# Reading and writing every helper matmul from the last column to the first

## The reference

```
x = x + 1/2 * SwiGLU_1(RMSNorm(x))                       # width 2816
h = RMSNorm(x)
[qA|kA|vA|c_q|c_kv|k_rope|gate_A|gate_B] = h @ w_in      # 1184 columns and two gates of 1024
oA = sliding-window attention, 8 heads of 64, 2 key heads, ALiBi, a sink per head
oB = latent attention, 8 heads, query rank 256, key/value rank 128, rotary part of 32
x = x + (sigmoid(gate_A)*(oA @ w_branch_a) + sigmoid(gate_B)*(oB @ w_branch_b)) @ w_out
x = x + 1/2 * SwiGLU_2(RMSNorm(x))
```

## Time and profile before

| what | value |
|---|---|
| median of the runs | 1039.09 us (1038.88 to 1039.29) |
| the profiled execution's own time | 1040.34 us |
| its span, first to last instruction | 1038.5 us |
| TensorE busy with matmuls (PE) | 1032.4 us, 99%, 5648 records |
| TensorE weight loads (PEld, beside PE) | 891.7 us, 86%, 5648 records |
| VectorE (DVE) | 718.3 us, 69% |
| ScalarE (ACT) | 586.1 us, 56% |
| GpSimd (POOL) | 61.8 us, 6% |
| DMA | 187.53 MB, mean 181 GB/s, 51.0% of 16 engines on the main queue |
| granted TensorE clock, mean | 1.000 |

### The profile page before, as it was taken

The page is one execution under the profiler, slowest core; times in us unless marked ns, Lnnn a source line. Parts: engine busy times, 40 slices in busy tenths (PEclk is TensorE's granted clock), DMA queues, the critical chain, the costliest instruction groups (busy, mean ns, idle before and its releaser), DMA issues.

```text
span 1038.5 us, 15559 instructions
## 1 busy us (share of the span) xinstructions
PE 1032.4 (99%) x5648; PEld 891.7 (86%) x5648; DVE 718.3 (69%) x1132; ACT 586.1 (56%) x935; POOL 61.8 (6%) x71
## 2 busy tenths in 40 slices
PE   8999999999999999999999999999999999999998
PEld 7888888998888888888888888889988888888887
DVE  6766666668786876666687666666688868666665
ACT  6555454466963754554565455455678646454552
POOL 0052000121100000000000000001211000000000
PEclk9999999999999999999999999999999999999999
DMA  7665544455435455655445555534454346545541
GB/s 264 248 225 192 204 162 167 140 183 193 146 123 203 173 187 189 205 189 209 179 147 202 202 192 182 210 136 152 154 203 163 122 163 219 205 163 202 191 173 61
DMA packets 35269, 187.53 MB, mean 181 GB/s; under 512 B 4368, under 2 KB 4384, under 8 KB 20128
## 3 DMA queue, kind: packets, MB, share of 16 engines
q1 hardware_dynamic: 34992, 186.51, 51.0%
q0 software_dynamic: 240, 0.53, 0.2%
HBM read 185.98 MB, written 1.05 MB: 180 GB/s over the span
## 4 chain that ended last, share of the span: by engine, by line
PE 99%; DMA 1%; SPq 0%; DVE 0%; ACT 0%; issue 0%
PE ps L1369 96%; PE ps L1803 1%; PE ps L1393 1%; DMA w_raw<-in_w_ffn 1%; PE ps L1832 1%; PE ps L1868 0%; PE ps L1712 0%; PE ps L1704 0%; PE ps L1414 0%; DVE x_cols L999 0%; ACT w_hi L554 0%; SPq L318 0%; SPq L317 0%
## 5 line engine op out<-in xcount | busy, mean ns | idle before, releaser
L1369 PE MATMUL ps<-hT,w_hi 128*128 128x512 f32 x1408 | 341.3, 391 | 1.9 <-ACT w_hi L554 1.9
L1369 PEld LDWEIGHTS ps<-hT,w_hi 128*128 128x128 f32 x1408 | 258.9, 188 | 52.4 <-ACT w_hi L554 2.1
L884 DVE TENSOR_TENSOR w_lo<-w_raw,w_hi 128x2048 fp32r<-128x2048 f32 x82 | 188.0, 2293 | 87.7 <-ACT w_hi L549 87.7
L1369 PEld LDWEIGHTS ps<-hT,w_lo 128*128 128x128 f32 x1408 | 176.8, 188 | 7.5
L1369 PE MATMUL ps<-hT,w_lo 128*128 128x256 f32 x1408 | 178.3, 279 | 0.0
L1369 PE MATMUL ps<-w_hi,hT 128*128 128x512 f32 (+2 forms) x576 | 174.3, 377 | 0.0
L549 ACT ACTIVATE w_hi<-w_raw 128x2048 fp32r<-128x2048 f32 x85 | 162.0, 1906 | 13.9 <-PE ps L1369 13.2
L1369 PE MATMUL ps<-w_lo,aTh 128*128 128x512 f32 x352 | 137.2, 390 | 0.0
L1369 PE MATMUL ps<-w_hi,aTl 128*128 128x512 f32 x352 | 137.0, 389 | 0.0
L1369 PE MATMUL ps<-w_hi,aTh 128*128 128x512 f32 x352 | 136.8, 390 | 0.0
L578 ACT ACTIVATE S<-ps 128x256 f32<-128x256 f32 x88 | 33.7, 383 | 154.6 <-PE ps L1369 154.6
(11 more groups left out here) (168 smaller groups left out, 952.9 us busy)
## 6 DMA issues: line engine op xcount, KB each, us to landing
w_raw<-in_w_ffn SPq DMA_DIRECT2D x85, 1024.0 KB, 4.9
w_raw<-in_w_ffn SPq DMA_DIRECT2D x90, 512.0 KB, 5.7
w_raw<-in_w_gate SPq DMA_DIRECT2D x16, 1024.0 KB, 5.1
w_raw<-in_w_proj SPq DMA_DIRECT2D x16, 592.0 KB, 4.4
w_raw<-in_w_branch SPq DMA_DIRECT2D x8, 1024.0 KB, 4.8
w_raw<-in_w_out SPq DMA_DIRECT2D x8, 1024.0 KB, 4.8
w_raw<-in_w_uq SPq DMA_DIRECT2D x4, 384.0 KB, 3.0
w_raw<-in_w_ffn SPq DMA_DIRECT2D x4, 256.0 KB, 6.6
```

What stands on the lines that cost most here:

```text
L884: dve.tensor_tensor(wl_gu[b], raw_gu[b], wh_gu[b].bitcast(F32), ALU.subtract).then_inc(lo_gu.sem, 1)
L1369: return pe.matmul(dst, w, m, start=start, stop=stop, skip_group_check=True)
```

## The change

The helper gives both the output and the moving operand with their columns in descending order. Column j of the moving operand still yields column j of the output, so each output element is the same sum; the stationary operand, the flags, the order of the matmuls and all waits are as before.

```diff
             def mm(dst, w, m, start, stop):
-                return pe.matmul(dst, w, m, start=start, stop=stop, skip_group_check=True)
+                return pe.matmul(dst[:, ::-1], w, m[:, ::-1], start=start, stop=stop, skip_group_check=True)
```

## The result

The changed kernel takes 1059.96 us (1059.67 to 1060.25) where the kernel before takes 1039.09 (1038.88 to 1039.29): a ratio of 1.0198, with a 95% interval of 1.0181 to 1.0215. That is 20.9 us slower. The forecast of no change was wrong. The time lies inside the range, but only because the range took in the second rival, a small price at each matmul.

A forecast was written before the change was run, and what follows sets the result against it. TensorE, busy in 99% of the span, was taken to bound the kernel. Read, write and fixed price summed as 0 + 0 + 0 on the median of 1039.09, giving 1039.1 us, with a range of 1035 to 1111 us.

The forecast's parts named there:

- the second rival: At each matmul, a small fixed price such as a refetch at the far end: 1075 us at 7 ns, 1111 at 14; chance 0.12.
- The bound: Whole kernel: TensorE, busy in 99% of the span, sets the time; any change per helper matmul arrives in full.
- Step (a): Helper matmuls' moving operand read downwards from SBUF: taken as zero, since aligned groups of neighbouring words stay complete.
- the third rival: In the matmul stream, turned order avoids a clash with weight load or other engines' writes: 28 us gain at most, 1011 us; chance 0.04.
- Step (b): Helper matmuls writing and adding downwards in PSUM: taken as zero, upper bound 0.35 ns more a column.
- The rule set against it: PSUM writes: lines hold two float32 values and non-contiguous patterns slow matmuls significantly; if step -1 counts, the sum is about 1820 us.
- Step (c): Fixed price per matmul for a start at the far end: taken as zero, 0 to 14 ns kept for the range.
- The first: At every helper matmul, descending SBUF reads or PSUM writes are not merged, each column its own access: about 1820 or 1930 us; chance 0.16.
- The fourth: In the build, both sides could be put back into ascending order, so nothing changes: 1039 us; chance 0.05, within the 0.68.

The follow-up runs named there:

- read_only: Kernel before, with only the moving operand read in descending column order and the output written upwards: 1060.17 us, ratio 1.0194.
- pairs_turned: Full kernel, moving operand and output upwards in pairs of columns, only the two columns of each pair swapped: 1039.52 us, ratio 1.000.
- quads_down: Full kernel, moving operand and output in groups of four columns in descending order, ascending inside each group: 1060.62 us, ratio 1.0202.
- write_only: Kernel before, with only the output written in descending column order and the moving operand read upwards: 1039.91 us, ratio 1.0001.
- micro_shift: Small kernel of 48-matmul sections, stationary operand shifted by 0 to 128 columns, then moving by 4, 32, 120; 512 up at stationary shift 64: 227.7 ns.
- micro_scan: Small kernel of 48-matmul sections, stationary operand shifted by 0 to 60 columns in steps of 4; 512 up: 226.7 ns at shift 0, 227.3 at 60.

## Why the prediction was wrong, step by step

**The bound** was right. TensorE passed every nanosecond on: 5000 float32r matmuls, no cover, no new wait.

**Step (a), the read, failed.** It was taken as zero and is the whole of the 20.9 us (read_only alone, 1.0194). The ground for zero was geometry: aligned groups stay whole. The runs support the half of it that concerns the inside of a group (pairs_turned, 1.000). But the order in which the groups are visited has a price (quads_down, 1.0202), and the argument looked at the moving stream alone. What it left out is the place of the stationary operand, and with it, by inference, the second read of the same engine, the weight load of 188 ns that runs beside each matmul. Rival 2 mentioned it as reading the same memory in its own order; that half sentence named what the runs on place point at, and the rival got 0.12 because it was argued away by the fixed part being alike for all operands. By the sizes in the code it was alike because the operands of all 512-wide matmuls lie at the same distance modulo 64 columns.

**The slope and the fixed part were misread.** From 227 and 117 ns I drew 0.43 ns a column and 7 ns fixed. With both operands at shift 0, the sections at 256, 320, 384 and 512 columns give 120.0, 146.7, 173.3 and 226.7 ns, which is width/2.4 + 13.3 ns each time. So between these widths a column costs the clock's 0.417 ns, the fixed part is 13.3 ns, and the 256-wide matmuls of the full kernel, which lie at shift 120, take 116.9 ns and so lie 3.1 ns below that line. My line through two widths mixed two places. The excess of a column over the clock, on which the third rival's 28 us rested, was a misreading. It is no law for every width either: 448, 480 and 496 columns take 202.7, 216.7 and 223.5 ns, 2.7 to 3.5 above the line, which stays unexplained.

**Step (b), the write,** was right at zero: write_only 1.0001. The rule set against it, from the Trainium skill (Advanced Engine Details and Errata, PSUM Cachelines), doesn't apply to a step of -1 here.

**Step (c), the fixed price,** was taken as zero and bounded at 14 ns. It isn't one price: 6.3 ns at 512 columns, 4 to 5 at 384 and 416, 0.6 at 256, none for plain float32. The sum by this: 3256 x 6.3 = 20.5 us, 336 x 4.3 = 1.4, 1408 x 0.6 = 0.8, together 22.7 us against 20.4 in the pieces of the chain. It overshoots because not every upward matmul was fast in the kernel before. The twelve down products behind a 256-wide group took 510.12 - 507.37 = 2.75 us there, 229.2 ns each, and each piece of twelve between two groups of transposes grew only from 2.76 to 2.81 us, 4 ns a matmul. The example price of 7 ns for all 5160 instructions had given 36 us.

**The rivals.** The first, that each column becomes an access of its own, fell: at 320 columns both directions take 146.7 ns. The third, a gain by avoiding a clash, had the object that the runs on place point at and the wrong sign: if there is a clash, the upward order is the one that avoided it. At 256 columns and shift 0, downward reading does gain (120.0 to 118.3). The fourth fell with the result.

**What is shown and what isn't.** Shown: the price is in the read, VectorE and ScalarE have no part, and upward reading pays the same price when either of TensorE's two operands is moved by a few columns, with one section that did not (shift 4 in micro_shift). That the two reads meet in the same part of SBUF is the inference from this; no trace shows a port or a bank. That downward reading pays for the same reason is inferred too, from the same 233 ns and from prices that don't add. Why downward reading has no good place, and why blocks of 64 columns escape, was not settled. In which order the weight load reads was not tried.

## What to carry to other kernels

Where TensorE is the bound, the two operands of a matmul stream have a good and a bad relative place in SBUF, here with a period of 64 float32 columns, as far as tried, and worth 2% of the time. An edit that adds a small buffer, changes a slot's padding or turns a read order can lose that without touching the work, so note the step between starts before and after each edit of the layout. Read a fixed cost per matmul from three widths or more, all at the same place of the operands.

## What was not expected of the hardware

The Trainium skill (SBUF — State Buffer, Who interferes with whom) gives TensorE two independent read ports and says that it never waits on anyone. As to VectorE and ScalarE the runs agree: 10.88 and 11.21 us a section, idle or busy. The Trainium skill (TensorE: Matmul & The Clock Gate, Step-by-step: what each phase is for) also says that loading the next weights doesn't steal read bandwidth from the running matmul. That is hard to square with the measurements, though no run shows where the two reads would meet: moving the stationary operand by 4 columns takes a 512-wide matmul from 226.7 to 233.3 ns in micro_scan. In micro_shift the same section took 226.9, so the state in which a stream settles also depends on what ran before it.

PSUM writes in descending order, accumulation included, are free (write_only, 1.0001), and a negative step on the moving operand is free where only neighbours in a pair change place (pairs_turned, 1.000).
